# Both pairs of down blocks by seven products in a row, each behind its phase's eight long halves

## The chip, the cores and the metric

The kernel runs on one core of a Trainium2 chip. The metric is the device time of one execution in microseconds (us), lower is better. In this text PE is TensorE, DVE is VectorE, ACT is ScalarE, POOL is GpSimd and SP is SyncE.

## The reference, cut to what matters

The reference is a trunk of two layers on 256 tokens of width 2048. Each layer has a mixer (pooling beside latent attention), a gated feed-forward part and a gated per-layer embedding. The change touches the feed-forward part and the seam behind it:

```python
def conv_gated_ffn(x, w_up, conv_w, conv_b, w_down):      # D_FF = 5632
    gu = x @ w_up                                          # 2048 x 11264
    gate, up = gu[..., :D_FF], gu[..., D_FF:]
    gate = causal_depthwise_conv(gate, conv_w, conv_b)     # three taps along the tokens
    return (jax.nn.silu(gate) * up) @ w_down               # 5632 x 2048
...
    h = h + conv_gated_ffn(rms_norm(h, norm_ffn_g[i]), ...)
    gate = jax.nn.sigmoid(rms_norm(h, norm_ple_g[i]) @ w_ple_gate[i])
    h = h + (p[i] @ w_ple[i]) * gate
```

Everything is float32.

## The kernel before, in words

**Precision.** PE works on float32r. Each operand is split in a high and a low part, and three products stand for one: high x high, low x high, high x low (`three`, lines 1901 to 1903). So every weight that is loaded must be split before PE can use it.

**Weights.** SP loads weights as chunks of 1 MB (128 partitions x 2048 values) into 4 slots of `raw`. A chunk is used as two halves of 1024 columns. For every half, ACT writes `w_hi` (a copy that rounds, line 996 or 722), then DVE writes `w_lo = raw - w_hi` (line 1566 or 1181), then PE multiplies. `w_hi` and `w_lo` have 6 slots. The engines' programs are written out by hand: while PE works on half n, ACT and DVE are at half n+4 (`AHEAD`), and neither can write half m before PE has used half m-6 (`w_used`). `go(a, b)` in the programs of ACT and DVE stands for the splits of halves a+4 to b+3.

**The feed-forward part** goes by units of 512 of the 5632 columns: 11 units, the first written out, ten in a loop that holds two. A unit has 27 halves:
- 8 long halves for the gate and 8 for up (`by_rows`). The weights are the stationary operand. One long half is 8 products of 512 columns (w_hi against both parts of x) and 8 of 256 columns (w_lo against the high part). The gate's four tiles go to the PSUM banks `acc`, up's to the four banks of `tps`.
- 11 short halves for down: 512 rows of w_down, four blocks of 512 output columns. Two blocks (columns 1024 to 2047) are taken together as a 2 x 2 matrix by Strassen's scheme in Winograd's form: seven products instead of eight, of sums of corners of the activation (`s_sums`) and of the weights (`t_sum`, in place in `raw`). Four halves are made from two chunks a second time, so that these two chunks give seven halves. Each product is 6 matmuls of 512 columns. The other two blocks (PLAIN_0, PLAIN_1) are multiplied plainly: 48 matmuls.

The down part of unit u-1 stands behind the gate and up part of unit u, so that ACT and DVE have time for what lies between. ACT copies the low part of the gate and up banks to SBUF and does the SiLU; DVE adds (`gate_sum`, `up_sum`), scales (`gate_normed`), does the three taps of the convolution (`tap_2`, `tap_1`, `tap_0`) and the product of gate and up (`gated`).

**What becomes of the products.** DVE reads each from its PSUM bank (`product_added`): three go straight to the residual `h` (`by_token`, line 1536, with the row's factor), four are added to sums in SBUF that go on through all units (`sum_p1`, `sum_p7`, `sum_p6`, `sum_p5`, line 1691). The two plain blocks are added to `h` too, two tiles each. After the last unit these sums are combined (`corners_summed`, line 1768) and added to `h` in `add_block` for blocks 2 and 3.

**The seam.** Unit 10's own down part follows plainly (halves from `M_DOWN`). After each of its four blocks `add_block` finishes 512 columns of `h`. PE waits for `h_ready` of block j behind the first half of block j+1 (of block 2 behind the second half of block 3) and turns `h` for the next stage by transposes (`turn_h`, line 1958). POOL makes the low part of the last activation (line 669).

## Time and profile before

| | |
|---|---|
| median of 3 runs | 2156.09 us (2156.04 to 2156.51) |
| the profiled execution | 2156.12 us |
| its span in the trace | 2154.3 us |
| PE busy | 2141.7 us (99% of the span) |
| DVE busy | 1707.6 us (79%) |
| ACT busy | 1125.1 us (52%) |
| POOL busy | 50.4 us (2%) |
| granted PE clock | 0.999 |

The span is the time from the first to the last instruction in the trace; the execution's own time is 1.8 us longer. Matmuls are pipelined: a row gives each 0.39 us, but they start 0.227 us apart, so paces below are taken from start to start. DVE's and ACT's instructions overlap a little in the same way.

### The profile page before, as it was taken

To read this page: it belongs to the slowest core of one execution; us is meant where nothing else is said; L and a number is where in the kernel's file an instruction comes from. 1 tells how busy PE (TensorE), PEld (TensorE's weight loads), DVE (VectorE), ACT (ScalarE), POOL (GpSimd) and SP (SyncE) were. 2 spreads that over 40 slices of the span, in tenths; PEclk is the share of its full clock that TensorE was granted. 3 is DMA by queue.
4 is the path that set the end of the run, shared out by engine and by line. 5 is a ranking of instruction groups with operands and counts; after the bars stand their busy time and mean duration, and the time that the engine had idled before them with its cause. 6 is when DMAs were issued, how large, how long until landed. Compare 5 with 4: busy or idle time off the path is not lost.

```text
span 2154.3 us, 32719 instructions
## 1 busy us (share of the span) xinstructions
PE 2141.7 (99%) x11526; PEld 1859.3 (86%) x11526; DVE 1707.6 (79%) x2192; ACT 1125.1 (52%) x1422; POOL 50.4 (2%) x114
## 2 busy tenths in 40 slices
PE   9999999999999999999999999999999999999998
PEld 8898888888888888888898988888888888888886
DVE  5797569888889888897557875788888889888964
ACT  6556445554555544555554664445544545544554
POOL 2000000000000000000000000000000000000011
PEclk9999999999999999999999999999999999999999
DMA  8645555546555546555556455555556555556562
GB/s 269 213 139 174 178 200 188 182 158 233 205 204 178 182 166 234 197 192 195 173 183 182 138 176 176 201 203 176 186 177 234 195 197 176 183 185 234 176 216 97
DMA packets 233323, 406.75 MB, mean 189 GB/s; under 512 B 14828, under 2 KB 50268, under 8 KB 233096
## 3 DMA queue, kind: packets, MB, share of 16 engines
q1 hardware_dynamic: 231976, 402.72, 55.0%
q0 software_dynamic: 512, 1.76, 0.2%
q10 hardware_dynamic: 736, 1.07, 0.1%
q8 instruction: 48, 0.79, 0.1%
q14 instruction: 51, 0.42, 0.1%
HBM read 403.42 MB, written 2.10 MB: 188 GB/s over the span
## 4 chain that ended last, share of the span: by engine, by line
PE 97%; ACT 1%; DVE 1%; issue 1%; POOL 0%; POOLq 0%; DVEq 0%; ACTq 0%
PE acc L2082 16%; PE tps L2082 16%; PE acc L1901 12%; PE acc L1903 12%; PE acc L1902 12%; PE tps L2092 9%; PE acc L2092 9%; PE tps L1902 3%; PE tps L1903 3%; PE tps L1901 3%; PE acc L1988 1%; PE tps L1958 1%; ACT sq_h L773 0%; DVE h L1536 0%; DVE xb_lo L1193 0%
## 5 line engine op out<-in xcount | busy, mean ns | idle before, releaser
L996 ACT ACTIVATE w_hi<-raw 128x1024 fp32r<-128x1024 f32 x540 | 559.2, 1058 | 536.3 <-PE acc L2092 116.6
L1566 DVE TENSOR_TENSOR w_lo<-raw,w_hi 128x1024 fp32r<-128x1024 f32 x540 | 650.2, 1225 | 161.5 <-ACT w_hi L996 149.8
L1181 DVE TENSOR_TENSOR w_lo<-raw,w_hi 128x1024 fp32r<-128x1024 f32 (+1 forms) x288 | 342.0, 1211 | 143.2 <-ACT w_hi L722 137.6
L722 ACT ACTIVATE w_hi<-raw 128x1024 fp32r<-128x1024 f32 (+2 forms) x287 | 290.2, 1044 | 179.5 <-PE acc L1903 126.3
L2082 PE MATMUL acc<-xa,w_hi 128*128 128x512 f32 x1536 | 366.0, 391 | 0.0
L2082 PE MATMUL tps<-xa,w_hi 128*128 128x512 f32 x1536 | 361.2, 390 | 0.0
L2082 PEld LDWEIGHTS tps<-xa,w_hi 128*128 128x128 f32 x1536 | 285.3, 188 | 57.2
L2082 PEld LDWEIGHTS acc<-xa,w_hi 128*128 128x128 f32 x1536 | 283.7, 188 | 56.2 <-DVE h L1521 0.4
L1902 PE MATMUL acc<-w_hi,xb_lo 128*128 128x512 f32 x640 | 249.0, 389 | 0.0
L1901 PE MATMUL acc<-w_hi,xb_hi 128*128 128x512 f32 x560 | 220.5, 394 | 0.4 <-ACT pw L1072 0.4
L1903 PE MATMUL acc<-w_lo,xb_hi 128*128 128x512 f32 x560 | 218.1, 389 | 0.0
L2092 PEld LDWEIGHTS acc<-xa,w_lo 128*128 128x128 f32 x1536 | 192.7, 191 | 5.1
L2092 PE MATMUL acc<-xa,w_lo 128*128 128x256 f32 x1536 | 194.2, 283 | 0.0
L2092 PEld LDWEIGHTS tps<-xa,w_lo 128*128 128x128 f32 x1536 | 190.6, 192 | 3.7
L2092 PE MATMUL tps<-xa,w_lo 128*128 128x256 f32 x1536 | 191.8, 283 | 0.0
L1902 PEld LDWEIGHTS acc<-w_hi,xb_lo 128*128 128x128 f32 x640 | 120.3, 188 | 24.0
L1903 PEld LDWEIGHTS acc<-w_lo,xb_hi 128*128 128x128 f32 x560 | 105.1, 188 | 22.1
L1901 PEld LDWEIGHTS acc<-w_hi,xb_hi 128*128 128x128 f32 x560 | 105.2, 188 | 21.6 <-issue 0.8
L1582 DVE TENSOR_TENSOR raw<-raw 128x1024 f32<-128x1024 f32 x80 | 97.8, 1222 | 0.7
L1901 PE MATMUL acc<-w_hi,gt_hi 128*128 128x512 f32 x240 | 93.4, 389 | 0.0
L1902 PE MATMUL acc<-w_hi,gt_lo 128*128 128x512 f32 x240 | 93.4, 389 | 0.0
L1903 PE MATMUL acc<-w_lo,gt_hi 128*128 128x512 f32 x240 | 93.4, 389 | 0.0
(262 smaller groups left out, 2651.1 us busy)
## 6 DMA issues: line engine op xcount, KB each, us to landing
raw<-in_w_up SPq DMA_DIRECT2D x176, 1024.0 KB, 5.0
raw<-in_w_down SPq DMA_DIRECT2D x88, 1024.0 KB, 5.0
raw<-in_w_out SPq DMA_DIRECT2D x32, 1024.0 KB, 5.0
raw<-in_w_ple_gate SPq DMA_DIRECT2D x32, 1024.0 KB, 5.1
raw<-in_w_in SPq DMA_DIRECT2D x21, 1024.0 KB, 5.4
raw<-in_w_ukv SPq DMA_DIRECT2D x8, 1024.0 KB, 5.5
raw<-in_w_in SPq DMA_DIRECT2D x8, 864.0 KB, 4.8
raw<-in_w_uq SPq DMA_DIRECT2D x6, 1024.0 KB, 5.7
```

Source lines behind the costliest of these rows:

```text
L722: copy(w_hi[:, half_of(m), 0:n], raw[:, c % RAW_SLOTS, at:at + n], ACT.Copy).then_inc(hi_done, 1)
L996: copy(w_hi[:, half_of(m), :], raw[:, c % RAW_SLOTS, half * HALF:(half + 1) * HALF], ACT.Copy).then_inc(hi_done, 1)
L1181: dve.tensor_tensor(w_lo[:, half_of(m), 0:n], raw[:, c % RAW_SLOTS, at:at + n], w_hi[:, half_of(m), 0:n].bitcast(F32), ALU.subtract).then_ ...
L1566: dve.tensor_tensor(w_lo[:, half_of(m), :], raw[:, slot, half * HALF:(half + 1) * HALF], w_hi[:, half_of(m), :].bitcast(F32), ALU.subtract ...
L1582: dve.tensor_tensor(dst, a, b, ALU.subtract).then_inc(t_made, 1)
L1901: pe.matmul(dst, a_hi, b_hi, start=first, stop=False)
L1902: pe.matmul(dst, a_lo, b_hi, start=False, stop=False)
L1903: return pe.matmul(dst, a_hi, b_lo, start=False, stop=last)
L1958: ins = pe.transpose(bank[:, i * S + t * P:i * S + (t + 1) * P], tiles(t, i), ident[:, :])
L1988: ins = pe.matmul(acc[BL["cq"] % 2][:, t, :], a[:, 2 * k + i, t * P:(t + 1) * P], w[:, cols], start=first, stop=last)
L2082: ins = pe.matmul(dst, hi[:, k * BLK + n * P:k * BLK + (n + 1) * P], x_both[:, kt, :, :].rearrange("p a s -> p (a s)"), start=kt == 0, sto ...
L2092: ins = pe.matmul(bank(n, False)[:, S:2 * S], lo[:, k * BLK + n * P:k * BLK + (n + 1) * P], xa[0][:, kt, :], start=False, stop=False)
```

## The change

The unit now has 30 halves in two phases of 15. A phase is 8 long halves (the gate's in the first, up's in the second) and then 7 products in a row, for one pair of down blocks: columns 0 to 1023 behind the gate, 1024 to 2047 behind up. No block of a unit is plain any more, but for unit 10's own down part. In detail:
- PE: 14 products of 6 matmuls in place of 7 products and 48 matmuls. The first phase's products go to `tps`, the second's to `acc`, each bank but one twice. `x_half` orders the first long half of a phase by bank, and waits there until ACT (`staged`) and DVE (`h_taken`) have read the last products.
- ACT copies four products of each phase to `stage` (`take`), and does `tap_2` in place of DVE. `up_low` moves from behind up's halves to the start of the next unit.
- POOL adds the four staged products of each phase to the sums in SBUF by accumulating DMAs (`products_added`), 8 a unit.
- DVE adds the other three of each phase to `h` (`from_bank`), 6 a unit, and makes the corner sums of the weights for both pairs.
- The loop holds one unit. The last unit is written out apart (`ends`): its up_sum and gated stand in it, before its second phase's T3, and four `corners_summed` too. DVE makes the low part of the last activation in place of POOL.
- In the seam `add_block` of blocks 0 and 1 now adds corner sums as well, and PE waits at `M_DOWN` for banks of the last products.

The diff, cut to its core:

```diff
-ACC_UNIT = 6
-JOB_UNIT = 12
-TURN_UNITS = 2
+ACC_UNIT = 2
+JOB_UNIT = 4
+TAKES, KEEPS = 4, 3
...
+        T_ORDER = (T1, T3, T2, T4)
+        TAKEN = (B11, T1, T3, T2, T4)[0:TAKES]
+        KEPT = (B21, B22, T4)[0:KEEPS]
+        BY_BANK = ((0, 3), (0, 0), (0, 1), (1, 3), (1, 0), (1, 1), (0, 2), (1, 2))
...
 # POOL
-                pool.tensor_tensor(xa[1][:, 0:4, :], conv[:, :, :], xa[0][:, 0:4, :].bitcast(F32),
-                                   ALU.subtract).then_inc(g_lo, 1)
+                def products_added(v, second):
+                    p1, p7, p6, p5 = sums[second]
+                    for i, dst in enumerate((p1, p5, p7, p6)):
+                        pool.wait_ge(staged, taken(l, v, second, i + 1))
+                        pool.sem_inc(stage_seen, 1)
+                        pool.dma_start(dst, stage[:, second, i, :], accum_op=ALU.add).then_inc(added, 16)
+                    pool.wait_ge(added, 16 * TAKES * phases(l, v, second))
+                    pool.sem_inc(stage_free, 1)
...
 # ACT
+                    def take(second, k, bank, scale=1.0):
+                        halves_used(act, l, M_UNIT + PHASE * second + FORM_AT + k, v)
+                        if k == B11:
+                            act.wait_ge(stage_free, phases(l, v, second))
+                        copy(stage[:, second, TAKEN.index(k), :], bank, ACT.Copy, scale=scale).then_inc(staged, 1)
+                    up_low(u - 1, lambda: halves_used(act, l, M_UNIT - 1, v))
+                    go(0, 2)
+                    act.wait_ge(g_done, UNITS * l + u)
+                    copy(gt[0][:, :, :], conv[:, :, :], ACT.Copy).then_inc(g_hi, 1)
+                    go(2, 5)
...                     s_hi
+                    go(5, 10)
+                    take(0, B11, tps[:, 0, :])
+                    go(10, 13)
+                    take(0, T1, tps[:, 3, :])
+                    go(13, 14)
+                    take(0, T3, tps[:, 0, :])
+                    go(14, 15)
+                    take(0, T2, tps[:, 1, :])
+                    gate_low(lambda: halves_used(act, l, M_UNIT + 7, v))
+                    go(15, 17)
+                    tap_2(u)
+                    go(17, 23)
+                    silu(u)
+                    if not ends:
+                        go(23, 25)
+                        take(1, B11, acc[0][:, 0, :])
+                        go(25, 28)
+                        take(1, T1, acc[1][:, 1, :])
+                        go(28, 29)
+                        take(1, T3, acc[0][:, 0, :])
+                        go(29, 30)
+                        take(1, T2, acc[0][:, 1, :])
+                        return
...
 # DVE
+                    go(0, 1)
+                    up_sum(u - 1)
+                    gated(u - 1)
+                    go(1, 3)
+                    s_sums(v, 0)
+                    s_sums(v, 1)
+                    go(3, 4)
+                    dve.wait_ge(g_hi, UNITS * l + u)
                     lo(gt[1][:, :, :], conv[:, :, :], gt[0][:, :, :]).then_inc(g_lo, 1)
+                    s_sums(v, 2)
+                    s_sums(v, 3)
                     go(4, 5)
+                    t_sum(v, 0, 1)
+                    t_sum(v, 0, 2)
...                     s_lo
+                    go(5, 7)
+                    t_sum(v, 0, 3)
+                    t_sum(v, 0, 4)
+                    go(7, 11)
+                    from_bank(0, B21, tps[:, 1, :])
+                    go(11, 12)
+                    from_bank(0, B22, tps[:, 2, :])
+                    go(12, 15)
+                    from_bank(0, T4, tps[:, 2, :])
+                    go(15, 16)
                     gate_sum(u, 0)
                     gate_sum(u, 1)
                     gate_normed()
-                    go(10, 11)
-                    tap_2(u)
+                    go(16, 18)
                     tap_1(u)
+                    go(18, 19)
                     tap_0(u)
+                    go(19, 20)
+                    if ends:
+                        corners_summed(0, 0)
+                        corners_summed(0, 1)
+                    t_sum(v, 1, 1)
+                    t_sum(v, 1, 2)
+                    go(20, 22)
+                    t_sum(v, 1, 3)
+                    t_sum(v, 1, 4)
+                    if not ends:
+                        go(22, 26)
+                        from_bank(1, B21, acc[0][:, 1, :])
+                        go(26, 27)
+                        from_bank(1, B22, acc[1][:, 0, :])
+                        go(27, 30)
+                        from_bank(1, T4, acc[1][:, 0, :])
+                        return
+                    go(22, 24)
+                    corners_summed(0, 2)
+                    corners_summed(0, 3)
                     up_sum(u)
+                    gated(u)
+                    go(24, 26)
+                    from_bank(1, B21, acc[0][:, 1, :])
+                    dve.wait_ge(g_hi, UNITS * l + UNITS)
+                    lo(xa[1][:, 0:4, :], conv[:, :, :], xa[0][:, 0:4, :]).then_inc(g_lo, 1)
                     go(26, 27)
+                    from_bank(1, B22, acc[1][:, 0, :])
+                    go(27, 30)
+                    from_bank(1, T4, tps[:, 2, :])
...
 # PE
+                    for i in range(8):
+                        x_half(i, i, gate_acc, v)
+                    pe.wait_ge(t_done, JOBS * l + JOB_UNIT * v + (j0 + T_BANKS))
+                    pe.wait_ge(g_lo, UNITS * l + u)
+                    product(0, B11, tps[:, 0, :])
+                    product(0, B21, tps[:, 1, :])
+                    pe.wait_ge(s_split_lo, (UNITS - 1) * l + u)
+                    product(0, B22, tps[:, 2, :])
+                    product(0, T1, tps[:, 3, :])
+                    pe.wait_ge(staged, taken(l, v, 0, 1))
+                    product(0, T3, tps[:, 0, :])
+                    pe.wait_ge(h_taken, kept(l, v, 0, 1))
+                    product(0, T2, tps[:, 1, :])
+                    pe.wait_ge(h_taken, kept(l, v, 0, 2))
+                    product(0, T4, tps[:, 2, :])
+                    for i in range(8):
+                        x_half(PHASE + i, i, up_acc, v)
...                     the same seven for the second pair, in acc
+                    pe.wait_ge(t_done, JOBS * l + (JB["p"] + T_BANKS))     # the last unit's T3, T2, T4, in tps
...
                 m, b = M_DOWN, BL["ple"] - N_BLK
                 pe.wait_ge(g_lo, UNITS * l + UNITS)
+                pe.wait_ge(staged, taken(l, UNITS - 2, 1, 2))
+                pe.wait_ge(h_taken, kept(l, UNITS - 2, 1, 2))
                 for j in range(N_BLK):
                     for i in down(m + 2 * j, b + j, xa):
                         if i == 0 and j == 0:
                             pe.wait_ge(p_landed, 16 * l + 16)
+                            pe.wait_ge(staged, taken(l, UNITS - 2, 1, TAKES))
+                            pe.wait_ge(h_taken, kept(l, UNITS - 2, 1, KEEPS))
                             turn(l, JB["p"], lambda t, n: p_tok[:, t, n * P:(n + 1) * P])
```

## Rows read from the trace of the kernel before

**Rows 1.** The page: span, busy engines, and the chain that ended last.

```profile
span 2154.3 us, 32719 instructions
PE 2141.7 (99%) x11526; PEld 1859.3 (86%) x11526; DVE 1707.6 (79%) x2192; ACT 1125.1 (52%) x1422; POOL 50.4 (2%) x114
...
PE 97%; ACT 1%; DVE 1%; issue 1%; POOL 0%; POOLq 0%; DVEq 0%; ACTq 0%
```

**Rows 2.** Busy time in one unit: window, total, PE, PEld, DVE, ACT, POOL.

```profile
694.04:758.90 64.86, 64.86 (x347) 56.28 (x347) 56.05 (x67) 32.65 (x34) 0.00 (x0) 1.00 0.56 194
```

**Rows 3.** Timeline of PE: start us, us; first gate, down, next gate.

```profile
692.52 3.79 PE L2082 MATMUL acc<-xa,w_hi 128*128 128x512 f32 x16
...
736.97 0.39 PE L1901 MATMUL acc<-w_hi,gt_hi 128*128 128x512 f32 x1
...
757.37 3.79 PE L2082 MATMUL acc<-xa,w_hi 128*128 128x512 f32 x16
```

**Rows 4.** Timeline of DVE in that unit: start us, us.

```profile
715.57 0.69 DVE L1601 TENSOR_TENSOR gate_f<-acc,gate_f 128x512 f32<-128x512 f32 x1
...
717.49 1.23 DVE L1566 TENSOR_TENSOR w_lo<-raw,w_hi 128x1024 fp32r<-128x1024 f32 x1 [0.30 <-DVE gate_f L1601]
...
721.75 1.38 DVE L1613 TENSOR_SCALAR conv<-gate_f,prm_all 128x256 f32<-128x256 f32 x4
...
724.18 1.67 DVE L1620 SCALAR_TENSOR_TENSOR conv<-gate_f,prm_all,conv 128x255 f32<-128x255 f32 x4
...
732.91 2.48 DVE L1582 TENSOR_TENSOR raw<-raw 128x1024 f32<-128x1024 f32 x2
...
742.50 0.69 DVE L1691 TENSOR_TENSOR corner<-acc,corner 128x512 f32<-128x512 f32 x1
743.11 0.74 DVE L1536 SCALAR_TENSOR_TENSOR h<-acc,rstds,h 128x512 f32<-128x512 f32 x1
743.76 2.35 DVE L1566 TENSOR_TENSOR w_lo<-raw,w_hi 128x1024 fp32r<-128x1024 f32 x2
```

**Rows 5.** Timeline of ACT, same columns.

```profile
714.94 1.09 ACT L1033 ACTIVATE gate_f<-acc 128x512 f32<-128x512 f32 x2 [0.75 <-PE acc L2082]
...
738.09 2.94 ACT L996 ACTIVATE w_hi<-raw 128x1024 fp32r<-128x1024 f32 x3
...
961.20 1.57 ACT L736 ACTIVATE xb_hi<-tps,prm_all 128x256 fp32r<-128x256 f32 x4 [0.31 <-PE tps L1958]
```

**Rows 6.** Timeline: ACT's copies from PSUM, and a matmul that waited for them.

```profile
982.32 2.06 ACT L1072 ACTIVATE pw<-acc 128x512 f32<-128x512 f32 x4
983.55 0.47 PE L1901 MATMUL acc<-w_hi,xb_hi 128*128 128x512 f32 x1 [0.19 <-ACT pw L1072]
```

**Rows 7.** DMA: landing times of unit weights; a load of 256 KB by POOL.

```profile
DMA to landing us min/median/max: 4.8/5.0/7.1
...
p_tok<-in_p POOLq DMA_DIRECT2D x2, 256.0 KB, 4.8
```

**Rows 8.** Timelines around POOL's instructions: an arithmetic one, a DMA.

```profile
948.79 2.94 POOL L669 TENSOR_TENSOR xa<-conv,xa 128x1024 fp32r<-128x1024 f32 x1 [664.52 <-ACT xa L1049]
950.70 2.12 DVE L1566 TENSOR_TENSOR w_lo<-raw,w_hi 128x1024 fp32r<-128x1024 f32 x1
...
2053.13 0.61 POOL L676 DMA_DIRECT2D fin_g<-in_final_norm_g  x1
2051.92 2.35 DVE L1181 TENSOR_TENSOR w_lo<-raw,w_hi 128x1024 fp32r<-128x1024 f32 x2
```

**Rows 9.** Timeline of the seam: h_ready's work on DVE, PE's transposes.

```profile
958.06 1.40 DVE L1536 SCALAR_TENSOR_TENSOR h<-acc,rstds,h 128x512 f32<-128x512 f32 x2
960.56 1.03 PE L1958 MATMUL tps<-ident,h 128*128 128x128 f32 x8
...
972.63 1.40 DVE L1536 SCALAR_TENSOR_TENSOR h<-acc,rstds,h 128x512 f32<-128x512 f32 x2
974.07 1.41 DVE L1536 SCALAR_TENSOR_TENSOR h<-corner,rstds,h 128x512 f32<-128x512 f32 x2
```

More of the change, by code:

```diff
@@ L424, in scalar_of, with phases @@
+        def phases(l, v, second):
+            return 2 * (UNITS - 1) * l + 2 * v + (second + 1)
         def scalar_of(col):
@@ new lines, in up_low, with tap_2 @@
+                def up_low(u, used):
+                    used()
+                    act.wait_ge(conv_done, UNITS * l + u + 1)
+                    copy(up_f[:, :, :], tps[:, :, S:2 * S], ACT.Copy).then_inc(up_lo, 1)
+                def tap_2(u):
+                    act.wait_ge(gate_step, 3 * UNITS * l + 3 * u + 3)
+                    for ft in range(4):
+                        copy(conv[:, ft, :], gate_f[:, ft, :], ACT.Identity,
+                             bias=prm[:, bass.ds(4 * u + (BIAS + ft), 1)],
+                             scale=prm[:, bass.ds(4 * u + (TAP[2] + ft), 1)]).then_inc(tap_done, 1)
@@ L1009, in first_unit @@
-                    steps(l, m0 + 13, m0 + 16)
-                    halves_used(act, l, m0 + 15)
-                    copy(up_f[:, :, :], tps[:, :, S:2 * S], ACT.Copy).then_inc(up_lo, 1)
-                def unit(l, w, i):
-                    u = TURN_UNITS * w + (i + 1)
-                    m0 = M_UNIT + i * UNIT_HALVES
+                    gate_low(lambda: block_ready(act, l, BL["ffn"]))
+                    steps(l, m0 + 9, m0 + 11)
+                    tap_2(0)
+                    steps(l, m0 + 11, m0 + 13)
@@ new lines, in unit @@
+                    go(23, 24)
+                    up_low(u, lambda: halves_used(act, l, M_UNIT + PHASE + 7, v))
+                    go(24, 25)
+                    take(1, B11, acc[0][:, 0, :])
+                    go(25, 26)
+                    act.wait_ge(g_done, UNITS * l + UNITS)
+                    copy(xa[0][:, 0:4, :], conv[:, :, :], ACT.Copy).then_inc(g_hi, 1)
+                    go(26, 28)
+                    take(1, T1, acc[1][:, 1, :])
+                    go(28, 29)
+                    take(1, T3, tps[:, 0, :])
@@ L1051, in _ @@
+                    go(29, 30)
+                    take(1, T2, tps[:, 1, :])
+                first_unit()
+                with act.Fori(1, UNITS - 1) as u:
+                    unit(u, u - 1, False)
+                unit(UNITS - 1, UNITS - 2, True)
                 d0 = M_DOWN
@@ L1674, in first_unit, with corners_summed @@
                     steps(l, m0 + 15, m0 + 16)
-                    up_sum(0)
-                    gated(0)
-                def unit(w, i):
-                    u = TURN_UNITS * w + (i + 1)
-                    m0 = M_UNIT + i * UNIT_HALVES
+                def corners_summed(second, k):
+                    p1, p7, p6, p5 = sums[second]
+                    dst, src = ((p6, p1), (p7, p6), (p6, p5), (p5, p7))[k]
+                    if k == 0:
+                        dve.wait_ge(stage_free, phases(l, UNITS - 2, second) + 2)
+                    else:
+                        dve.wait_ge(corner_folded, 8 * l + 4 * second + k)
+                    dve.tensor_tensor(dst, dst, src, ALU.add).then_inc(corner_folded, 1)
@@ L2393, in unit, with product, bank_taken @@
                     s4, s1, s3, s2 = ((s_hi[:, k], s_lo[:, k]) for k in range(4))
+                    left = {B11: a11, B21: a12, B22: s4, T1: s1, T3: s3, T2: s2, T4: a22}
+                    def product(second, k, bank):
+                        corner_product(M_UNIT + PHASE * second + FORM_AT + k, v, left[k], bank)
+                    def bank_taken(second, f):
+                        if f == 2:
+                            pe.wait_ge(h_taken, kept(l, v, second, 0))
+                        else:
+                            pe.wait_ge(staged, taken(l, v, second, {3: 2, 0: 3, 1: 4}[f] - TAKES))
@@ L2409, in _ @@
+                    pe.wait_ge(t_done, JOBS * l + (JB["p"] + T_BANKS))
+                    product(1, T3, tps[:, 0, :])
+                    product(1, T2, tps[:, 1, :])
+                    product(1, T4, tps[:, 2, :])
                 jobs_split(l, JB["ffn_norm"] + 5)
                 first_unit()
-                with pe.Fori(0, LOOPS) as w:
-                    for i in range(TURN_UNITS):
-                        unit(w, i)
+                with pe.Fori(1, UNITS - 1) as u:
+                    unit(u, u - 1, False)
```

391 lines of the change are left out of this document (189 added, 202 removed).

## The prediction

> **What bounds the kernel now.** I began with the page. PE is busy for 2141.7 of 2154.3 us, and 97% of the chain that ended last is PE's [rows 1], so what shortens PE's work shortens the time, as long as nobody else becomes late. Next came the windows of one unit: 64.86 us, all PE's; DVE works 56.05 us of them, ACT 32.65 [rows 2]. So DVE has 8.8 us to give in a unit, and ACT plenty. Then I read the timelines. PE's unit runs from 692.52 to 757.37: 44.45 us for 16 long halves, 2.78 each, and 20.40 us for 90 short matmuls, 0.2267 each [rows 3]. Ten such units stand in each layer, 20 in all.
>
> **What PE saves.** 14 products x 6 = 84 matmuls in place of 90: 6 x 0.2267 = 1.36 us a unit, 27.2 us in all. The unit's work is then 64.85 - 1.36 = 63.49 us, a phase 31.74. With nothing else the profiled execution would go from 2156.1 to 2128.9 us (it stands 0.03 us above the median of the runs, so I take the two as one).
>
> **What DVE gets.** A split takes 1.22 us, and two in a row 2.35: neighbours overlap by 0.09, so one costs 1.13 [rows 4]. Added a unit: 3 splits, 3.4 us; four more corner sums, of which two in a row take 2.48, or 2.40 with the overlap, 4.8. Removed: tap_2, 1.38 - 0.09 = 1.3; four adds to the corner sums at 0.60, 2.4; one of seven adds to h, 0.65. All in [rows 4]. Net +3.85: 59.9 of 63.5 us, 94%. It fits in sum, with 3.6 us to spare, so the question is what DVE waits for, and I walked through a unit. ACT: a split starts every 0.94 us and is finished after 1.06; a `take` costs 0.50; tap_2's four pieces, by the four scaled pieces of the same width, about 1.4 [rows 5]. ACT's second copy from a bank ended at about 983.4 and PE's matmul followed at 983.55 [rows 6]: I take 0.20 from a release to PE's start, and as much from PE's last matmul to the reader.
>
> **First phase.** Time 0 is the end of PE's last product. ACT can only now do up_low (0.2), and split 4 behind it is ready at 2.2. DVE, which is done with its last bank at about 1.2, starts split 4 at 2.2, up_sum 3.3, gated 4.6, split 5 at 5.7. ACT had to wait for gated with g_hi (5.9), so split 6 is ready only at 7.85: DVE idles for 1.0 us. From here it has no gap: s_sums, splits 7 and 8 with g_lo and the other s_sums between, corner sums from 13.9, s_lo 16.3, splits 9 and 10, two corner sums, splits 11 to 14 from 22.1 to 26.7, then B21's bank, split 15, B22's bank (28.4), splits 16 to 18, and T4's bank at 32.5, finished at 33.2. PE ends T4 at 31.74 and needs this bank for its seventh matmul, 6 x 0.2275 = 1.37 later (the order by bank puts it last), at 33.1. With 0.20 for the release PE stands for **0.32 us**. The other banks and splits are early: B21's is free 1.6 us ahead, split 14 over 3 us.
>
> **Second phase.** DVE: split 19 at 33.4, the gate sums (1.92 from 715.57 to 717.49 [rows 4]), normed finished at 37.65; ACT's tap_2 from 37.7 to 39.1 holds back split 21, ready at 40.2, and DVE idles 1.5. Then tap_1 (1.58), tap_0, splits and corner sums in a row up to split 28 at 56.1; T4's bank is finished at 65.1, and needed at 63.49 + 0.32 + 1.37 = 65.2. With the release this is 0.15 late, which does not add: the next phase's DVE chain starts from PE's end, and its 0.32 contains it. So a unit lasts 63.8 us, and 20 x 0.32 = **6.4 us** of the gain go. The moved steps issue nothing on SP's queue: its loads go by lo_done as before, and POOL's queue holds only the adds.
>
> **The last unit and the seam.** Here DVE gets four corners_summed (2.7), up_sum and gated (2.4), and g_lo (1.1), in the fullest stretch. In the walk split 27 is at 56.3, two corners_summed, up_sum 58.75, finished 60.0: T3 needed it at 59.7, and PE starts at 60.25 (0.5 late). Gated, then split 28, ready at 62.4: another 1.0. Split 29, B21's bank, g_lo (behind ACT's g_hi), split 30, B22's bank, finished at 67.1, for which PE waits at `M_DOWN`: 2.0. T4's bank stands behind splits 31 to 33 and is finished at 71.15, while PE wants to turn p at 70.0: 1.3. Then add_block of block 0 takes 2.9 us before h_ready instead of 1.4 (two more adds, as in 972.63 to 975.5), so h_ready is at 960.95 in the old clock, where PE turned at 960.56 [rows 9]: 0.4. Block 1's comes behind the low parts of the block before, which slid by as much, and again 1.4 longer: 1.5; block 2's 0.1. Together 6.85 us a layer, **13.7 us**. The cover of all this was DVE's slack; where it is gone each further us of DVE work in this stretch costs one. POOL's low part goes, with the 0.9 us by which it stretched a split (2.12 against 1.22 [rows 8]); that split hid, so nothing is gained.
>
> **The accumulating DMAs.** No row shows one. A load of 256 KB by POOL landed after 4.8 us [rows 7]. `stage` is asked for again two phases later, a phase lasts 32 us, so from nothing to 20 us each they hide; their issue (0.61 us on POOL for another load) left DVE's two splits at 2.35 [rows 8]. I take nothing for both.
> The Trainium skill, page "SBUF — State Buffer", section "Who interferes with whom", speaks against this change: DMAs that POOL generates in software write their descriptors through a port that VectorE can hold. By the row above no such loss is seen, though the issues there were single ones; by the page they could come late under a DVE that is busy 94%, which is the last rival below, there priced by a row.
>
> **Sum.** 27.2 - 6.4 - 13.7 = 7.1 us: 2156.1 - 7.1 = **2149.0 us**.
>
> **Rivals.**
> *VectorE keeps up.* PE's stalls are hidden, since each bank is late by tenths only and the walk adds some 30 numbers of +-0.02. For it: the lateness is 0.32; against it: the seam's, 1 to 2 us at a time. All hidden gives 2128.9; only the seam's left, 2142.6. Chance 0.15 for a time below 2141.
> *Gain and seam cancel.* The stalls in a unit are 0.45 to 0.85 rather than 0.32: 27.2 - 20 x 0.65 - 13.7 = 0.5, about 2155.6; the change then takes work from PE and leaves the time. 0.23.
> *The adds hold back a weight chunk.* The chunk of halves 19 and 20 can only be issued when split 13 is done (25.6) and ACT wants it at 32.3. At 5.0 us it is there at 31.0. The longest landing seen was 7.1 [rows 7], and now two or three adds of 256 KB (twice that, as the target is read too) fall in its time. Each us behind 32.3 delays split 19 and all of DVE's second phase; half of it, spread over both T4 waits, reaches PE: stall per unit (0.49 + d)/2. It decides from d = 0.87, a landing of 7.2 us. At 8.3 us (d = 2): 20 x 1.24 + 13.7 - 27.2 = 11.3, 2167.4. For it: the margin of 1.3 us; against it: the DMA engines are hardly more than half busy (0.56 [rows 2]). 0.20 for slower by this.
> The Trainium skill, page "DMA: Bandwidth & Descriptors", section "Issuing engines are not separate DMA queues", says that DMAs of all issuers run on the same 16 engines and interleave; by that the delay would be real, and only its size open.
> *POOL and DVE hold each other up.* POOL's instruction that read SBUF stretched a DVE split by 0.9 us [rows 8]. If each of 8 issues did so, DVE would have 59.9 + 7.2 = 67.1 us in a unit, over 64.86: at least 20 x 2.3 + 13.7 = 59 slower, 2215. Against it: the DMA issue left the splits alone. 0.05.
>
> **How the numbers follow.** A time between 2141 and 2151.8 has 0.37, as forecast; with the first rival 0.52 for faster by over 0.2% (4.3 us, about what a measurement of this kernel can tell from no change). Same: 0.23. Slower: 0.20 + 0.05. The range leaves out the fourth rival (0.05) and the ends of the first and third (0.12 together): 2133 to 2167. The forecast's own is 2141 to 2152.
>
> **What would show it.** PE: 84 matmuls of down in a unit, period near 63.8, with a gap of some 0.3 us behind the sixth matmul of up's first half, its releaser DVE's add to h from tps; in the last unit and the seam gaps of 0.5 to 2 us, whose releasers are up_sum, w_lo and h. DVE near 94%, with idle of 1.0 before split 6 and 1.5 before tap_1. Wrong would be: no gap behind the sixth matmul; ACT waiting for `raw` at split 19; DVE splits longer than 1.23 at POOL's issues; the seam without gaps. What I trust least is the order of small waits: a few tenths in every phase are 40 times that.

## The result

The changed kernel takes 2174.9 us (median; 2173.5 to 2175.28) beside 2156.24 us of the kernel before (2156.04 to 2156.51) on the same chip: a ratio of 1.0085, 95% interval 1.0068 to 1.0103. It is slower, by 18.7 us. The prediction said 2149.0 us and 2133 to 2167, with 0.25 for slower: it missed by 25.9 us, with the wrong sign, and the range did not hold the time.

### The profile page after: what moved, and what is told of

Read it like the earlier page. It is cut to its first block, busy times and chain, and to the rows that moved or that the text cites. A ratio compares the mean times of both kernels' runs of the same rounds, so it can differ in the third digit from the quotient of the medians.

```text
span 2173.1 us, 33763 instructions
## 1 busy us (share of the span) xinstructions
PE 2130.9 (98%) x11406; PEld 1831.9 (84%) x11406; DVE 1786.8 (82%) x2162; ACT 1295.6 (60%) x1730; POOL 183.4 (8%) x274
## 4 chain that ended last, share of the span: by engine, by line
PE 84%; DVE 8%; issue 4%; ACT 2%; DMA 1%; DVEq 0%; POOL 0%; POOLq 0%; ACTq 0%
PE acc L2474 13%; PE tps L2474 11%; PE acc L1984 10%; PE acc L1986 10%; PE acc L1985 10%; PE acc L2482 7%; PE tps L2482 6%; DVE w_lo L1657 4%; PE acc L2165 3%; PE tps L2165 3%; DVE h L1627 2%; PE tps L1986 2%; PE tps L1985 2%; PE tps L1984 2%; PE tps L2175 1%
## 5 line engine op out<-in xcount | busy, mean ns | idle before, releaser
L1657 DVE TENSOR_TENSOR w_lo<-raw,w_hi 128x1024 fp32r<-128x1024 f32 x600 | 711.5, 1218 | 99.0 <-ACT w_hi L1043 98.8
L1043 ACT ACTIVATE w_hi<-raw 128x1024 fp32r<-128x1024 f32 x600 | 615.4, 1056 | 290.6 <-DMA raw<-in_w_down 124.5
L2474 PE MATMUL tps<-xa,w_hi 128*128 128x512 f32 x1280 | 314.1, 392 | 13.9 <-DVE h L1627 13.9
L2474 PE MATMUL acc<-xa,w_hi 128*128 128x512 f32 x1280 | 313.7, 392 | 1.6 <-DVE h L1627 0.7
L2474 PEld LDWEIGHTS tps<-xa,w_hi 128*128 128x128 f32 x1280 | 233.7, 188 | 66.4 <-issue 19.4
L2474 PEld LDWEIGHTS acc<-xa,w_hi 128*128 128x128 f32 x1280 | 233.8, 188 | 53.5 <-DVE h L1627 9.2
L1672 DVE TENSOR_TENSOR raw<-raw 128x1024 f32<-128x1024 f32 x160 | 195.5, 1222 | 2.7
L708 POOL DMA_DIRECT2D corner_b<-stage x80 | 67.7, 846 | 611.1 <-ACT stage L1088 611.1
L708 POOL DMA_DIRECT2D corner<-stage x80 | 67.5, 847 | 597.7 <-ACT stage L1088 545.4
L1063 ACT ACTIVATE conv<-gate_f,prm_all 128x256 f32<-128x256 f32 x88 | 45.7, 590 | 80.4 <-DVE gate_f L1699 80.4
## 6 DMA issues: line engine op xcount, KB each, us to landing
raw<-in_w_down SPq DMA_DIRECT2D x88, 1024.0 KB, 11.2
```

What stands on the lines that cost most here:

```text
L708: pool.dma_start(dst, stage[:, second, i, :], accum_op=ALU.add).then_inc(added, 16)
L1043: copy(w_hi[:, half_of(m), :], raw[:, c % RAW_SLOTS, half * HALF:(half + 1) * HALF], ACT.Copy).then_inc(hi_done, 1)
L1657: dve.tensor_tensor(w_lo[:, half_of(m), :], raw[:, slot, half * HALF:(half + 1) * HALF], w_hi[:, half_of(m), :].bitcast(F32), ALU.subtract ...
L1672: dve.tensor_tensor(dst, a, b, ALU.subtract).then_inc(t_made, 1)
L2474: ins = pe.matmul(bank(f, kt == 0), hi[:, k * BLK + f * P:k * BLK + (f + 1) * P], x_both[:, kt, :, :].rearrange("p a s -> p (a s)"), start ...
```

## The profile after

The page of the changed kernel:

```profile
span 2173.1 us, 33763 instructions
PE 2130.9 (98%) x11406; PEld 1831.9 (84%) x11406; DVE 1786.8 (82%) x2162; ACT 1295.6 (60%) x1730; POOL 183.4 (8%) x274
...
PE 84%; DVE 8%; issue 4%; ACT 2%; DMA 1%; DVEq 0%; POOL 0%; POOLq 0%; ACTq 0%
...
raw<-in_w_up SPq DMA_DIRECT2D x176, 1024.0 KB, 5.8
raw<-in_w_down SPq DMA_DIRECT2D x88, 1024.0 KB, 11.2
...
corner_b<-stage POOLq DMA_DIRECT2D x80, 256.0 KB, 8.4
corner<-stage POOLq DMA_DIRECT2D x80, 256.0 KB, 8.0
```

PE has 120 matmuls fewer, as the edit says, and yet the span is 18.8 us longer. PE held 97% of the chain [rows 1] and now holds 84%; DVE has 8% of it. The busy share hardly tells: PE still reads 98%. A load of down's weights, which landed after about 5 us before [rows 7], takes 11.2 us at the median.

One unit, in the same view as [rows 2]; then the timelines of PE, DVE and ACT in it, as in [rows 3 to 5]:

```profile
627.69:692.49 64.80, 64.12 (x341) 54.96 (x340) 59.55 (x64) 40.98 (x48) 6.75 (x8) 1.00 0.75 227
```

```profile
627.69 2.38 PE L2474 MATMUL acc<-xa,w_hi 128*128 128x512 f32 x8
...
659.88 1.52 PE L2474 MATMUL tps<-xa,w_hi 128*128 128x512 f32 x6
...
661.97 0.72 PE L2474 MATMUL tps<-xa,w_hi 128*128 128x512 f32 x2 [0.56 <-DVE h L1627]
```

```profile
628.53 0.75 DVE L1627 SCALAR_TENSOR_TENSOR h<-acc,rstds,h 128x512 f32<-128x512 f32 x1
...
635.71 1.23 DVE L1657 TENSOR_TENSOR w_lo<-raw,w_hi 128x1024 fp32r<-128x1024 f32 x1 [0.94 <-ACT w_hi L1043]
...
641.36 1.23 DVE L1657 TENSOR_TENSOR w_lo<-raw,w_hi 128x1024 fp32r<-128x1024 f32 x1 [0.68 <-ACT w_hi L1043]
...
661.10 0.74 DVE L1627 SCALAR_TENSOR_TENSOR h<-tps,rstds,h 128x512 f32<-128x512 f32 x1
...
669.30 1.23 DVE L1657 TENSOR_TENSOR w_lo<-raw,w_hi 128x1024 fp32r<-128x1024 f32 x1 [2.18 <-ACT w_hi L1043]
```

```profile
640.26 1.06 ACT L1043 ACTIVATE w_hi<-raw 128x1024 fp32r<-128x1024 f32 x1 [3.63 <-DMA raw<-in_w_down]
...
666.24 2.08 ACT L1063 ACTIVATE conv<-gate_f,prm_all 128x256 f32<-128x256 f32 x4 [3.90 <-DVE gate_f L1699]
```

The unit should have shrunk to 63.49 us and lasts 64.80 here. Over nine units (starts at 303.55 and 887.74) it is 64.91, and 64.82 in the second layer, against 64.85 before: PE's saving is given back in full inside the loop. The place is where the prediction looked. Eight wide matmuls without a wait take 1.98 us, from start to the end of the last; the first gate half takes 2.38, and the first up half runs from 659.88 to 662.69, 2.81. So 0.40 and 0.83 us are lost, both behind the sixth matmul, both to DVE's add from T4's bank. With time 0 at 627.69, that add ends at 34.15 instead of 33.2. DVE's load is as computed (59.55 us, 59.9 in the prediction); what it lacks is not capacity but three inputs: it idles before split 6 (0.94; 1.0 was expected), before split 8 (0.68; not expected at all), and before split 21 (2.18; 1.5 was expected). Split 8 is late since ACT waits 3.63 us for its down chunk.

The waits of PE in the last unit and the seam of the first layer (all rows of its timeline from 945 to 1000 us that have a wait):

```profile
949.44 0.50 PE L1984 MATMUL tps<-w_hi,s_hi 128*128 128x512 f32 x1 [0.27 <-DVEq L1719]
951.90 0.50 PE L1984 MATMUL tps<-w_hi,s_hi 128*128 128x512 f32 x1 [0.80 <-DVE w_lo L1657]
956.78 0.47 PE L1984 MATMUL acc<-w_hi,xa 128*128 128x512 f32 x1 [1.87 <-DVE h L1627]
960.89 0.63 PE L2041 MATMUL tps<-ident,p_tok 128*128 128x128 f32 x4 [1.11 <-DVE h L1627]
967.29 1.09 PE L2041 MATMUL tps<-ident,h 128*128 128x128 f32 x8 [0.29 <-DVEq L1624]
976.64 1.09 PE L2041 MATMUL tps<-ident,h 128*128 128x128 f32 x8 [2.78 <-DVEq L1624]
993.77 0.47 PE L1984 MATMUL acc<-w_hi,xb_hi 128*128 128x512 f32 x1 [0.50 <-ACT pw L1161]
```

The first six answer, one by one, to the prediction's 0.5, 1.0, 2.0, 1.3, 0.4 and 1.5 us. They sum to 7.12 against 6.7 (in the second layer, where the sixth is 1.81, to 6.2). A row counts idle time from the modelled end of the matmul before, which lies later than the pace of 0.23 us would put the next start, so from start to start each of these waits is 0.16 to 0.28 us longer: 8.3 us in the first layer, 7.4 in the second. This walk held in its places and roughly in its sum, but for the sixth wait; the one inside the loop did not.

## The experiments

The theories. **A**: the accumulating DMAs hold back the down chunk, and with it ACT, split 8 and DVE. **B**: DVE's chain, with its waits for ACT's round trips (splits 6 and 21), is the bound of a unit. **C** and **D**: T4's bank is turned in the wrong place, either DVE reads it too late (C) or PE asks for it too early (D).

All runs in one table. "Unit" is the mean of nine, by PE's first gate matmuls, in the first and in the second layer. "Rest" is the time of the profiled execution less 2128.9 (all hidden) less ten times what each layer's unit has over 63.49; that is what the last units and seams cost, for which the prediction had 13.7. The profiled execution is within 0.7 us of the median but for run 4 (2166.41) and run 6 (2164.07). The ratios are each to runs of the kernel before on the same chip (2156.24 to 2156.45 us).

| kernel | median us | ratio to before, 95% interval | unit us, layer 1 and 2 | rest us |
|---|---|---|---|---|
| before | 2156.24 | 1 | 64.85, 64.85 | |
| changed | 2174.90 | 1.0085 [1.0068, 1.0103] | 64.91, 64.82 | 18.5 |
| 1 no adds | 2162.53 | 1.0029 [1.0017, 1.0040] | 64.46, 64.30 | 15.2 |
| 2 copies | 2164.79 | 1.0038 [1.0022, 1.0054] | 64.44, 64.31 | 18.1 |
| 3 T4 first | 2170.84 | 1.0067 [1.0045, 1.0089] | 64.94, 64.35 | 19.3 |
| 4 splits first | 2168.54 | 1.0058 [1.0040, 1.0076] | 64.59, 64.51 | 16.3 |
| 5 late bank | 2168.74 | 1.0057 [1.0039, 1.0075] | 64.41, 64.42 | 21.3 |
| 6 both orders | 2161.36 | 1.0023 [1.0013, 1.0033] | 64.19, 64.27 | 20.4 |
| 7 both, no adds | 2142.66 | 0.9936 [0.9918, 0.9954] | 63.56, 63.56 | 12.6 |
| 8 both, adds later | 2159.85 | 1.0021 [1.0009, 1.0033] | 63.56, 63.56 | 29.4 |
| 9 same, last unit mended | 2148.78 | 0.9965 [0.9952, 0.9979] | 63.56, 63.56 | 18.5 |
| 10 later adds alone | 2164.87 | 1.0039 [1.0024, 1.0054] | 64.46, 64.31 | 18.3 |
| 11 later adds, late bank | 2152.34 | 0.9980 [0.9970, 0.9989] | 63.77, 63.64 | 19.1 |
| 12 as 9, corners later | 2149.98 | 0.9969 [0.9958, 0.9980] | 63.56, 63.56 | 19.6 |

Runs 1, 2 and 7 do not give the reference's output: in runs 1 and 7 the sums of the staged products stay zero, in run 2 they hold the last product alone.

### 1 and 2: the adds left out, and as plain copies

```diff
-    pool.dma_start(dst, stage[:, second, i, :], accum_op=ALU.add).then_inc(added, 16)
-    pool.wait_ge(added, 16 * TAKES * phases(l, v, second))
```
```diff
-    pool.dma_start(dst, stage[:, second, i, :], accum_op=ALU.add).then_inc(added, 16)
+    pool.dma_start(dst, stage[:, second, i, :]).then_inc(added, 16)
```

> The changed kernel without its 160 accumulating DMAs (POOL still waits for the staged products and frees the stage; the corner sums stay zero, so that part of the result is left out). It took 2174.9 us, its units 64.9 where PE's work is 63.5. Theory A, the adds' traffic: they hold back the w_down chunks (11.2 us to land against 5.0 before), split 8 and with it all of VectorE; without them landing falls to 5 to 7 us, the 0.7 us idle before split 8 goes from every unit and 1.2 us from ScalarE's squares in each seam: about 2158. Theory B, VectorE's own chain is too long (it idles 0.9 us before split 6 and 2.2 us before split 21, whatever the DMAs do): units stay above 64.4, 2164 or more.

> The adds as plain copies of the same bytes on the same queue (the sums then hold only the last product, so that part of the result is wrong). It tells the accumulating from the moving. If reading the target and adding is what costs, the copies land in 3 to 5 us instead of 8, w_down chunks in 6 to 8 instead of 11.2, and the time is that without adds within 2 us. If any traffic at this moment costs as much, the time stays within 2 us of 2174.9.

Without the adds the kernel gains 12.4 us and is still slower than before; the time lies between what A (2158) and B (2164 or more) had said. A is real, and not enough. The copies move as many bytes without accumulating, and cost 2.3 us of these 12.4, none of it in the loop (64.44 us a unit). They also go in fewer packets, and POOL issues one in 0.54 us instead of 0.85. So what costs in the loop is accumulating, with the packets and the engine time that it takes. That it is not POOL's issues is shown by run 10 below, which has them all and run 1's unit. The text on the copies was a little too hopeful: they landed after some 6 us, not 3 to 5, and the time is 2.3 us above run 1's, not within 2. The DMA view from 430 to 880 us (seven units of the first layer; queue, packets, MB, share of 16 engines, then landing times) of the changed kernel and of run 2:

```profile
q0 software_dynamic: 7936, 14.42, 18.7%
...
raw<-in_w_down SPq DMA_DIRECT2D x28, 1024.0 KB, 11.3
```

```profile
q0 software_dynamic: 4480, 14.68, 8.6%
...
raw<-in_w_down SPq DMA_DIRECT2D x28, 1024.0 KB, 8.5
```

The same 14.5 MB hold the 16 engines for 18.7% of 450 us, 84 us, when they accumulate, and 39 us when they only move: with some 56 of them, 1.5 and 0.7 us each. ACT's waits for down's chunks over the whole run were 124.5 us with the adds, 24.3 with the copies and 1.0 without.

### 3 and 4: one order changed alone

```diff
-    go(12, 15)
+    go(12, 14)
     from_bank(0, T4, tps[:, 2, :])
+    go(14, 15)
```
```diff
-    go(0, 2)
+    go(0, 3)
     act.wait_ge(g_done, UNITS * l + u)
     copy(gt[0][:, :, :], conv[:, :, :], ACT.Copy).then_inc(g_hi, 1)
-    go(2, 5)
+    go(3, 5)
...
-    go(15, 17)
+    go(15, 18)
     tap_2(u)
-    go(17, 23)
+    go(18, 23)
```

(Run 3 has the same edit in the second phase.)

> VectorE reads T4's bank ahead of the last of the three splits behind it, in both phases of the looped units. Theory C, the order alone: the bank is then free in time, PE's two stalls a unit (0.4 and 0.8 us) go, units take 63.7: about 2152. Theory B, the chain: what stands behind T4 is now late by the same, the bank is reached 1.1 us earlier but the next phase starts no earlier; at best a third of the stalls goes: 2165 to 2170.

> Only ScalarE's order: split 6 ahead of g_hi (which waits for VectorE's gated) and split 21 ahead of tap_2 (which waits for gate_normed). Theory B: the two idle stretches of VectorE, 0.94 and 2.18 us a unit, go; the chain to T4's bank is 1 us shorter in the first phase and 3 in the second, so nearly all stalls in the units (1.4 each) and some 3 us in each last unit go: 2174.9 - 28 - 6 = 2141, faster than before. Theory A: split 8 still waits for its chunk, so the first phase gains nothing (VectorE idles there instead): stalls of 0.4 to 0.8 a unit stay, 2155 to 2160. Theory C: the bank stands where it stood; no more than 10 us gained.

Run 3 gains 4.1 us, less than either theory had said. A unit of the first layer gains nothing (64.94 us): the wait behind the sixth matmul shrinks, a new one of 0.45 us, released by another of DVE's adds to h, stands inside the products, and DVE's wait before split 8 grows from 0.68 to 1.92. In the second layer a unit gains 0.47 us, which over nine is all of the 4.1. C as the whole cause is out. Run 4 gains 6.4 us, where B had forecast 34 and A 15 to 20; only C's text (no more than 10) fits. DVE's waits before splits 6 and 21 are gone, it has two others of 1.57 and 1.54 us (0.68 and none before), and this stands on ACT at split 6 and at split 8:

```profile
631.63 1.06 ACT L1043 ACTIVATE w_hi<-raw 128x1024 fp32r<-128x1024 f32 x1 [2.35 <-DMA raw<-in_w_up]
638.59 1.06 ACT L1043 ACTIVATE w_hi<-raw 128x1024 fp32r<-128x1024 f32 x1 [4.00 <-DMA raw<-in_w_down]
```

The earlier ACT and DVE are, the more the late chunk holds them (3.63 us on ACT in the changed kernel, 4.00 here): the causes cover one another in part, and what removing one alone gives is not its price.

### 5 to 8: the bank asked for later, and the causes taken away together

```diff
-    if i % 2 == 0:
-        wide()
-        ins = narrow()
+    if i == 0:
+        for tiles in (BY_BANK[0:6], BY_BANK[6:8]):
+            wide(tiles)
+            ins = narrow(tiles)
+    elif i % 2 == 0:
+        wide(BY_ROW)
+        ins = narrow(BY_ROW)
```
```diff
 def products_added(v, second, wait=True):
+    if wait:
+        c = CH["ffn"] + 2 * (KT // 4) + PHASE_CHUNKS * (second + 1) + Q_CHUNK[0]
+        pool.wait_ge(raw_landed[c % RAW_SLOTS], l * (CHUNKS // RAW_SLOTS * 16)
+                     + v * (UNIT_CHUNKS // RAW_SLOTS * 16) + (c // RAW_SLOTS * 16 + 16))
```

The first is run 5; run 6 adds run 4's edit to it, run 7 leaves the adds out of run 6, and run 8 is run 6 with the second edit (`wait` is False for the last phase only). PE then wants T4's bank behind the sixth wide and the sixth narrow matmul, 2.08 us after its last product instead of 1.37.

> The first half of x in each phase does the wide and narrow products of tiles 3, 0 and 1 before those of tile 2, so that T4's bank is asked for some 0.7 us later; nothing else changes. Theory D (turn of T4's bank): part of PE's 0.4 us at each phase's first half is not VectorE's lateness but the way from PE's last product through VectorE's 0.75 us add back to PE, which without the adds still cost 2.2 to 2.4 us for eight wide products where 1.82 are work. Then 40 phases give back about 0.4 us each and up to 0.8 in the second: 2155 to 2163 against 2174.9. Theory B (VectorE's chain is the bound of a unit: 59.8 us of work and 5.1 of idle): VectorE's idles stay, PE only stands elsewhere, and the time stays within 3 us of 2174.9, with the stall now at the bank's new place and units still of 64.8 us.

> As the run before, and ScalarE makes split 6's high part before its copy of g and split 21's before tap_2. If VectorE's chain is the bound, the idles that go (0.9 and 2.2 us a unit) come through where ScalarE's weights have landed; the early splits alone gave 6.4 us, the two together should then give 10 to 20: 2155 to 2165. If the DMAs of the weights decide (theory A), ScalarE waits for raw as it did with the early splits alone, and the time stays at 2165 to 2169.

> As the run before, and the corner sums of the products are left out (these two sums keep only their first phase's or block's part, so the output is not the reference's). Theories A, B and D together: nothing of the three is left in a unit, units of about 63.6 us, the seam at some 6 us a layer: 2156.2 - 27.2 + 12 to 16 = 2141 to 2145. If units stay at 64.4 us as in the run without the adds, something that none of the three names holds PE.

> As the run with both orders, but POOL issues a phase's four adds only after the first down chunk of the phase behind it has landed, so that no add is under way while that chunk moves; the adds and their bytes are all still there. If what the adds cost is the delay of this one chunk, the time comes near that of the run without the adds (within 4 us). If they cost wherever they fall, since another chunk is then beside them, it stays near that of the run with both orders.

Run 5 gains 6.2 us, between its two theories. DVE's wait for split 8 grows from 0.68 to 1.16 us, since PE, and so the demand, is earlier. Run 6 gains 13.5, within its forecast and about the sum of runs 4 and 5 (12.5), and now ACT's wait for the down chunk is 5.01 us and DVE's before split 8 is 2.14:

```profile
637.04 1.06 ACT L1043 ACTIVATE w_hi<-raw 128x1024 fp32r<-128x1024 f32 x1 [5.01 <-DMA raw<-in_w_down]
638.14 1.23 DVE L1657 TENSOR_TENSOR w_lo<-raw,w_hi 128x1024 fp32r<-128x1024 f32 x1 [2.14 <-PE acc L2481]
```

Run 7 has none of the three, and a unit is 63.56 us: 0.07 from PE's own work. There the adds are worth 18.7 us, not the 12.4 of run 1. With the loop's stall and the adds gone, 2128.9 + 1.4 + 13.7 would be 2144.0, and 2142.66 was measured. So the saving and the seam were right to 1.3 us in sum, though not term by term: in run 7 PE has no wait for up_sum or split 28 in the last unit, where the walk had 0.5 and 1.0, and a stretch of lower clock instead (see the last section).

Run 8 has all the adds and still a unit of 63.56 us, so an add costs nothing in the loop if it isn't under way beside the down chunks. The time missed its forecast all the same (within 4 us of run 7), for it lost the gain in the last unit, where the adds of the first phase now waited for a chunk, and DVE for them, before its corner sums:

```profile
928.44 1.42 DVE L1770 TENSOR_TENSOR corner_b<-corner_b 128x512 f32<-128x512 f32 x2 [7.56 <-POOLq L714]
```

### 9 to 12: the last unit mended, and each part beside it

Run 9 is run 8 with `products_added(UNITS - 2, 0, False)`, so that the last unit's adds go out at once; run 10 has only its later adds, run 11 the later adds and the late bank. (The texts on record name splits 19 and 20 for the down chunk, after the prediction; the chunk in question is the one of splits 8 and 23. And where run 8's says that the adds wait for the first down chunk, the trace shows them go behind the second, which lands at 628.22 in run 9.)

> The run with the later adds had units of 63.56 us, as without the adds, but in the last unit the adds of its first phase waited for a chunk that lands only at 916, and VectorE stood 7.6 us for them before its corner sums, in each layer. Here the last unit's adds are issued as soon as their sums are staged; the rest is that run's. Theory A (the adds cost only through the down chunk that is late for splits 19 and 20): 2159.9 less 2 x 6 to 7.9, so 2144 to 2148, faster than the kernel before. If an add costs wherever it falls, something else takes over in the last unit: 2150 or more.

> The adds timed as in the run before, with the changed kernel's own orders (T4's bank, splits 6 and 21). All adds and their bytes are there. Theory A: within 2 us of the run without the adds, 2161 to 2165. If the bytes cost and not the late chunk: 2168 or more.

> The adds timed, and T4's bank asked for 0.7 us later; splits 6 and 21 as in the changed kernel. If the two waits of VectorE for ScalarE (0.9 and 2.2 us a unit) matter once the adds are out of the way, the time is 3 to 8 us above the run with all three: 2148 to 2155. If the bank's place alone was what remained, the two agree within 2 us.

> The run with all three, and two of the corner sums of the last unit (1.33 us of VectorE) are made after block 0 instead of ahead of up_sum. The prediction's seam: each us of VectorE's work ahead of the first block of the last part costs PE one, which waits there 1.9 us and then runs nine products at half the clock (0.43 instead of 0.23 us each). Then PE's wait there falls to 0.5 us, with the clock perhaps full behind it, and block 1 comes up to 1.3 us later: 1 to 5 us faster in all than the run with all three. If VectorE is full in the whole seam, the 1.3 us only move: within 1 us of it.

Run 9 takes 2148.78 us, 0.8 above its forecast, and is faster than the kernel before, by 0.35% (0.21 to 0.48%). Its loop, at the same stage as the changed kernel's unit above, and the landings of its whole run:

```profile
621.44:685.00 63.56, 63.56 (x341) 55.09 (x340) 59.74 (x64) 41.43 (x48) 6.92 (x8) 1.00 0.75 230
```

```profile
raw<-in_w_up SPq DMA_DIRECT2D x176, 1024.0 KB, 5.1
raw<-in_w_down SPq DMA_DIRECT2D x88, 1024.0 KB, 6.2
...
corner_b<-stage POOLq DMA_DIRECT2D x80, 256.0 KB, 4.7
corner<-stage POOLq DMA_DIRECT2D x80, 256.0 KB, 8.6
```

PE is busy for the whole 63.56 us, DVE for 59.74 (94%), and the DMA share is 0.75 as it was in the changed kernel: same work, same bytes, the same load on DVE, 1.3 us a unit less. What differs is when the adds are issued. The timelines of SP and POOL, of the changed kernel and of run 9 (the unit starts at 627.69 and 621.44):

```profile
626.60 2.62 SPq L582 DMA_DIRECT2D raw<-in_w_down  x2
...
620.98 0.85 POOL L708 DMA_DIRECT2D corner<-stage  x1 [24.86 <-ACT stage L1088]
...
627.85 0.84 POOL L708 DMA_DIRECT2D corner<-stage  x1 [0.59 <-ACT stage L1088]
```

```profile
620.22 2.62 SPq L582 DMA_DIRECT2D raw<-in_w_down  x2
...
628.86 3.46 POOL L712 DMA_DIRECT2D corner<-stage  x4 [28.01 <-DMA raw<-in_w_down]
```

SP issues the first of the two down chunks 1.1 us before the unit starts in one and 1.2 in the other, and the second 2.2 us behind it. Among the adds they take 11.0 and 11.3 us to land, ahead of them 5.2 and 5.8. In run 9 it is an up chunk, issued at 631.71 beside the adds, that takes 11.3 us, and no engine is seen to wait for it. Run 10 gives each unit as much as leaving the adds out did (64.46 us both, 64.31 and 64.30 in the second layer), so all that the adds cost in the loop is that the down chunks are late. Together with run 9: later adds 10.0 us, the late bank behind them 12.5 (run 11), the two early splits 3.6. In the other order (runs 4, 5, 6, 9) it was 6.4, 6.2, 13.5 for both orders, and 12.6 for the later adds.

The rest is 18.5 us in run 9 against 12.6 in run 7, so outside the loop the adds still cost some 6 us. The last unit's adds aren't held back, and its down chunk is late again. ACT and then DVE, in the first layer of run 9:

```profile
919.71 2.01 ACT L1047 ACTIVATE w_hi<-raw 128x1024 fp32r<-128x1024 f32 x2 [3.58 <-DMA raw<-in_w_down]
...
920.80 1.22 DVE L1661 TENSOR_TENSOR w_lo<-raw,w_hi 128x1024 fp32r<-128x1024 f32 x1 [1.17 <-ACT w_hi L1047]
```

Neither wait is in run 7, and nor is what follows, a wait of PE of 0.81 us at 937.73 for split 28 (in the second layer 0.78 for up_sum and 0.81 for split 28). The other part is at block 1, where PE waits 2.59 and 1.70 us in the two layers instead of 1.34, behind ACT's squares, which wait for POOL. From start to start these make 2.6 us of the 3.5 that the first layer's last unit and seam are longer than run 7's, and all of the 2.5 in the second layer.

Runs 10 and 11 came as forecast (11 is 3.6 us above run 9, so DVE's waits before splits 6 and 21 matter). Run 12 moved 1.33 us of DVE's corner sums behind block 0:

```diff
     go(22, 24)
-    corners_summed(0, 2)
-    corners_summed(0, 3)
...
+    if j == 1:
+        corners_summed(0, 2)
+        corners_summed(0, 3)
     add_block(l, bd + j, j, ((p1, p7), (p6, p5))[j])
```

Its timeline of PE, and run 9's behind it, at the first block of the last part and at block 1's transposes:

```profile
941.38 0.47 PE L1989 MATMUL acc<-w_hi,xa 128*128 128x512 f32 x1 [1.84 <-DVE h L1631]
...
963.17 1.63 PE L2046 MATMUL tps<-ident,h 128*128 128x128 f32 x8 [4.71 <-DVEq L1628]
```

```profile
942.61 0.59 PE L1988 MATMUL acc<-w_hi,xa 128*128 128x512 f32 x1 [1.88 <-DVE h L1631]
...
962.54 1.30 PE L2045 MATMUL tps<-ident,h 128*128 128x128 f32 x8 [2.59 <-DVEq L1628]
```

PE reaches the first block 1.2 us sooner, waits there as long as ever, and gives the time back at block 1, where it waits 2.1 us longer. The run is 1.2 us slower than run 9, just outside both of its theories and in the direction of no gain: in the seam DVE's work can be moved, but not hidden.

## Why the prediction was wrong

**What PE saves** held: 84 matmuls of down in a unit, and with nothing late a unit of 63.56 us (63.49).

**What DVE gets** held: 59.55 us in a unit (59.9).

**First phase** is the step that failed, with its result of 0.32 us a unit, where 1.42 were measured in the first layer (64.91 - 63.49) and 1.33 in the second. Ten of each less the 6.4 us of the sum is 21.1 of the 25.9 us that are missing. T4's bank was to be finished at 33.2 and was at 34.15. The walk gave split 8 no wait, since it never asked when its down chunk would land: 0.68 of the 0.95 us are that. 0.17 came from split 6, ready at 8.02 instead of 7.85. Without the adds (run 1) the bank still was finished at 33.8: DVE then waits 0.38 us for ACT before split 14, since ACT first copies B11's product, for which it waits for PE; the walk missed this. PE gave this turn 1.37 us from its last product, and DVE's add ended 1.96 us behind that product in the changed kernel and 1.52 in run 1; from its end to PE's start it took 0.13, not 0.20. Of the 1.35 us between the changed kernel's unit and run 9's, timing the adds took away 0.45 (run 10), asking for the bank later 0.69 (run 11) and the two early splits 0.21 (run 9), in this order.

**Second phase**: tap_2 on ACT took 2.08 us, not the 1.4 of the four scaled pieces, which made DVE's idle before split 21 2.18 instead of 1.5. The nearest row by shape was not near enough. That the gate half's lateness (0.40, by 0.15) doesn't add to the up half's held: T4's add ends at 34.15, PE could have asked at 33.11, and 0.40 of the difference had been spent at the gate half.

**The last unit and the seam** held in their places: 7.12 us by 6.7 and 6.2 in the second layer as the rows count idle time, 8.3 and 7.4 from start to start. The exception is block 1's turn (2.78 and 1.81 by 1.5): without the adds it is 1.34. The whole cost outside the units was 18.5 us by the table against 13.7, which is the other 4.8 of the 25.9 us, and 12.6 to 15.2 without the adds. The six waits of both layers are 15.7 of the 18.5 us from start to start; the other 2.8 were not traced one by one.

**The accumulating DMAs**, "I take nothing for both", is the second term at fault, and a part of the first. Their own latency hides, as stated. What doesn't is that two weight chunks are issued among them. With the orders as they are they cost 12.4 us, once the orders are mended 18.7.
The Trainium skill, page "DMA: Bandwidth & Descriptors", section "Issuing engines are not separate DMA queues", was cited for this delay being real if the transfers meet; the trace agrees (landing 11.2 us with the adds, 6.9 in run 1). The Trainium skill, page "SBUF — State Buffer", section "Who interferes with whom", was cited against the change for POOL's descriptors and VectorE. The prediction read it wider than it stands: the section also says that `tensor_tensor`, which DVE's splits are, takes only the read interface of the shared ports, while writing descriptors takes the write interface (marked there as inferred). Nor is this the fourth rival, which is about POOL slowing DVE. Here DVE's splits stayed at 1.22 us with eight issues of 0.85 us in a unit, and run 10, with all of the issues, has run 1's unit.

**The rivals.** The third, that the adds hold back a weight chunk, happened, but with another chunk: it named the one of halves 19 and 20, and it is down's, asked for by splits 8 and 23. Its condition was a landing of 7.2 us and its worst case 8.3; 11.2 came. Its price for a landing of 8.3 us, 2167.4, was 7.5 us short. The second, stalls of 0.45 to 0.85 us in a unit, is nearly the state without the adds: 0.97, and 2162.5 us. The two at once were not among the cases, though they don't exclude each other: both use up the same margin behind the sixth matmul. The first, VectorE keeping up, and the fourth, POOL and DVE disturbing each other, did not happen.

**Open**: the last 1 us or so of what the adds cost in the first layer's seam, which stretches of lower clock blur (last section); and why runs 5 and 6 have a rest of 21.3 and 20.4 us. The first has two such stretches in its first layer, the second one, and run 6's profiled execution is the slowest of its ten.

## What to carry to other kernels

Walk the DMA queue with the engines: for each chunk, when it can be issued, what is under way then, and when its first reader wants it. A transfer whose own latency hides can still cost through a load that moves beside it, and here a semaphore wait that let it go only after the critical chunks had landed took back all that it cost in the loop, with the same bytes. When several small waits use up one margin, take them all away in one run before pricing any: one at a time they gave 12.4, 6.4 and 6.2 us here (25.0 in sum), together 32.2.

## What the runs showed of the hardware

By the time of its packets, an SBUF-to-SBUF DMA that accumulates held the 16 DMA engines for 1.5 us per 256 KB, a plain one for 0.7. A chunk of 1 MB of down's weights landed after 11.2 us among such adds, after 8.5 among plain copies, and after 6.9 with neither (medians). POOL's issue took 0.85 and 0.54 us.

After a wait of 1.88 us at the first block of the last part, run 9's PE ran eight or nine matmuls at intervals of 0.43 instead of 0.23 us, with a granted clock (third column from the end) of 0.78 and 0.88 in the two windows around them. It is the 1.2 GHz level beside the 2.4 GHz one. After the wait of 2.59 us at block 1 it fell again, for seven more (0.83 in the windows from 960 to 970). In the changed kernel, which waited 1.87 and 2.78 us at the same places, it stayed at 1.00:

```profile
940.00:945.00 5.00, 3.12 (x10) 2.21 (x9) 5.00 (x6) 3.93 (x6) 2.53 (x3) 0.78 0.94 307
945.00:950.00 5.00, 5.00 (x23) 4.04 (x23) 4.04 (x5) 2.33 (x3) 0.00 (x0) 0.88 1.09 290
...
960.00:965.00 5.00, 2.46 (x12) 2.17 (x13) 4.01 (x6) 2.48 (x8) 0.00 (x0) 0.83 0.63 210
```

```profile
943.00 0.63 PE L1989 MATMUL acc<-w_hi,xa 128*128 128x512 f32 x1
943.43 0.63 PE L1990 MATMUL acc<-w_lo,xa 128*128 128x512 f32 x1
...
946.57 0.40 PE L1989 MATMUL acc<-w_hi,xa 128*128 128x512 f32 x1
```

The matmuls of the first fall take some 1.7 us longer (8.5 x 0.2). Most of it comes back: slower, PE reaches the transposes of p later, and the wait of 1.1 us for DVE there, which the changed kernel has at 960.89, is gone. Run 7 shows the net price: against the kernel before, its first layer's last unit and seam, with one fall (0.72 and 0.93), cost 0.4 us more than the second layer's, which has none and has the wait. In run 12, whose clock stayed at 1.00 at the first block, the wait is back as well (1.11 at 945.49). So a stall of PE can cost more than its length, but less than the slower matmuls suggest where another wait stands behind them. Why the clock falls in one kernel and not in another no run here tells.
